# Context mixer of layer 0 and latent mixer of layer 1: scans woven with independent projections, attention with three branches of the merge

## What is computed

```
def token_mixer(h, hc, ...):
    conv, ret, mls, att, gate = split_cols(h @ w_in)
    y0 = silu(layernorm(depthwise_conv(a * sigmoid(g), 31 taps)))
    y1 = head_norm(retention forward + backward) * silu(g)
    y2 = head_norm(mlstm forward + backward) * sigmoid(o)
    y3 = attention(q, k, v with the context's k, v and a sink)
    acc = sum_i sigmoid(gate_i) * (y_i @ w_branch[i])
    return acc @ w_out
```

## Time and profile before

| | |
|---|---|
| median of three runs | 6388.14 us (6384.92 to 6395.45) |
| span of the profiled execution | 6397.6 us |
| instructions | 64900 |
| TensorE matmul, VectorE, ScalarE, POOL busy | 65%, 50%, 11%, 43% |
| `c0`: convolution / up to attention blocks / attention blocks / first merge | 42 / 289 / 35 / 170 us |
| `l1`: convolution / up to attention blocks / attention blocks / first merge | 65 / 494 / 104 / 166 us |

### The profile page before, as it was taken

The page is one execution under the profiler, slowest core; times in us unless marked ns, Lnnn a source line. Parts: engine busy times, 40 slices in busy tenths (PEclk is TensorE's granted clock), DMA queues, the critical chain, the costliest instruction groups (busy, mean ns, idle before and its releaser), DMA issues. The chain is left out here.

```text
span 6397.6 us, 64900 instructions
## 1 busy us (share of the span) xinstructions
PE 4139.9 (65%) x23632; PEld 2474.1 (39%) x23632; DVE 3226.7 (50%) x7718; ACT 732.2 (11%) x1583; POOL 2759.8 (43%) x2606
## 2 busy tenths in 40 slices
PE   5789646667899785554454567887986743434447
PEld 3568523333566665221111114555875620000001
DVE  4321499755511585756645306444137866564440
ACT  1220101111210011000000001133110100000000
POOL 0000023555532144777777750000003577777775
PEclk8899877877999888665555578989998955555555
DMA  6445346789788499999999981110457999999999
GB/s 217 164 155 168 119 141 199 252 322 324 283 284 274 158 327 327 377 366 378 380 390 407 403 325 55 42 43 16 136 164 249 338 375 367 404 366 393 403 401 382
DMA packets 721231, 1739.23 MB, mean 272 GB/s; under 512 B 88912, under 2 KB 371408, under 8 KB 719248
## 3 DMA queue, kind: packets, MB, share of 16 engines
q0 software_dynamic: 380032, 1384.49, 57.1%
q1 hardware_dynamic: 314896, 304.03, 15.2%
q10 hardware_dynamic: 25984, 46.56, 2.0%
HBM read 1706.98 MB, written 27.89 MB: 271 GB/s over the span
## 5 line engine op out<-in xcount | busy, mean ns | idle before, releaser
L2692 POOL DMA_INDIRECT arena<-in_peer_u,arena x1280 | 1414.7, 1105 | 2519.1 <-DVE arena L1838 1245.0
L1081 PE MATMUL bank<-arena 128*32 128x256 f32 x10240 | 1202.3, 564 | 1372.1 <-DMA arena<-in_peer_v,arena 1366.4
L1940 DVE CUSTOM_DVE_ANT_0 arena<-arena 128x1024 f32<-128x1024 f32 x1280 | 1541.2, 1223 | 922.3 <-DMA arena<-in_peer_u,arena 907.5
L2692 POOL DMA_INDIRECT arena<-in_peer_v,arena x1280 | 1318.4, 1030 | 622.7 <-issue 319.2
L1081 PEld LDWEIGHTS bank<-arena 128*32 128x32 f32 x10240 | 251.9, 131 | 2270.8 <-DMA arena<-in_peer_v,arena 2173.8
L620 PE MATMUL bank<-arena 128*128 128x512 f32 (+1 forms) x1856 | 723.6, 549 | 109.4 <-issue 81.7
L989 PE MATMUL bank<-arena 128*128 128x256 f32 x2560 | 621.6, 399 | 156.0 <-issue 75.5
L989 PEld LDWEIGHTS bank<-arena 128*128 128x128 f32 x2560 | 508.9, 201 | 251.0 <-issue 152.2
L620 PEld LDWEIGHTS bank<-arena 128*128 128x128 f32 x1856 | 377.0, 207 | 436.1 <-issue 412.2
L995 PE MATMUL bank<-arena 128*128 128x256 f32 x1280 | 305.7, 382 | 0.0
L1042 PE MATMUL bank<-arena 128*128 128x256 f32 x1280 | 288.7, 389 | 19.4 <-issue 16.9
(11 more groups left out here) (265 smaller groups left out, 3900.9 us busy)
## 6 DMA issues: line engine op xcount, KB each, us to landing
arena<-in_w_in SPq DMA_DIRECT2D x152, 1024.0 KB, 6.9
arena<-in_mod_w POOLq DMA_DIRECT2D x20, 2048.0 KB, 11.5
arena<-in_peer_wq SPq DMA_DIRECT2D x40, 1024.0 KB, 6.0
arena<-in_w_branch SPq DMA_DIRECT2D x60, 512.0 KB, 6.6
arena<-in_w_out SPq DMA_DIRECT2D x20, 1024.0 KB, 7.8
arena<-in_peer_u,arena POOLq DMA_INDIRECT x1280
arena<-in_peer_v,arena POOLq DMA_INDIRECT x1280
arena<-in_w_branch SPq DMA_DIRECT2D x40, 256.0 KB, 8.5
```

The source lines that it names most:

```text
L1081: i = mm(banks[6 + g // 2][32 * j:32 * j + 32, (g % 2) * W:(g % 2 + 1) * W], G["ws"][:, g, 32 * m:32 * m + 32], G["row"][ROW_BUFFER["v", i ...
L1940: v.tensor_tensor_reduce(u, u, G["h2"][it % 2], 1.0, 0.0, ALU.mult, ALU.add, G["dots"][:, n:n + 1]).then_inc(*pr.step("dot", it, n))
L2692: fl.done(eng.indirect_dma_start(G["row"][x], None, table, bass.IndirectOffsetOnAxis(ids[:, n:n + 1], 0)), f"row_landed{x}", (kind + "_lan ...
```

## The change

Two passes, `c0` and `l1`, get another order (`woven`). New regions of the arena (`lay_low`, `lay_odd`, `GR_TOP`, `H2R_TOP`) let work of neighbouring stages lie side by side: both heads' projections, both mLSTM halves, attention inputs beside the last scan, and the merge's accumulator beside attention. The stages `ret1`, `rows` and `mls1` no longer exist there; their work belongs to the scan stage in which it is woven. Taps come in groups of four a row tile (8 instructions) instead of eight in `conv_tail`. `attn` is split into its inputs and its blocks, and the merge of the first half into the three branches that need no attention output and the fourth.

```
+WOVEN = ("c0", "l1")
...
 def pass_stages(p):
+    if woven(p):
+        s = ["norm", "conv", "ret0", "rets0", "rets1", "mlss0", "mlss1", "attn"]
+        return s + [f"{x}{f}" for f in range(len(halves_of(p))) for x in ("merge", "out", "query")]
...
+def weave(a, b, per):
+
+    due = 0.0
+    for cost in a:
+        yield cost
+        due += per
+        while due >= 1.0:
+            due -= 1.0
+            for cost in b:
+                yield cost
+                break
+    yield from b
...
+def units(p):
+
+    nb, rotated = p.n // P, 1 if p.t0 else 0
+    return dict(ret=12 + nb + 4 * rotated, scan=2 * nb + 4, mls=13 + nb, rows=2 + ROWS_LATER + nb, attn_in=9 + nb + 5 * rotated,
+                attn_mix=4 * nb + 2, merge=48)
...
+def merge_parts(p, f):
+
+    every = [(j, i) for j in range(D // W) for i in range(4)]
+    if woven(p) and f == 0:
+        return [x for x in every if x[1] < 3], [x for x in every if x[1] == 3]
+    return [every]
+
+
+def tap_parts(p):
+
+    return [(0, x) for x in range(4, 8)] + [(1, x) for x in range(8)] if woven(p) else \
+        [(0, 2), (0, 3), (1, 0), (1, 1), (1, 2), (1, 3)]
...
             def ret(p, h):
-                mn.stage((f"ret{h}", p.name))
+                if h == 0 or not woven(p):
+                    mn.stage((f"ret{h}", p.name))
...
             def normed(p):
+                if woven(p):
+                    yield from conv(p)
+                    u = units(p)
+                    taps = conv_tail(p)
+                    yield from weave(first(taps, 8), ret(p, 0), u["ret"] / 8)
+                    yield from weave(ret_scan(p, 0), weave(taps, ret(p, 1), u["ret"] / 7), (u["ret"] + 7) / u["scan"])
+                    yield from weave(ret_scan(p, 1), weave(rows(p), mls(p, 0), u["mls"] / u["rows"]), (u["mls"] + u["rows"]) / u["scan"])
+                    yield from weave(mls_scan(p, 0), mls(p, 1), u["mls"] / u["scan"])
+                    yield from weave(mls_scan(p, 1), attn_in(p), u["attn_in"] / u["scan"])
+                    yield from weave(attn_mix(p), merge_part(p, 0, merge_parts(p, 0)[0]), u["merge"] / u["attn_mix"])
+                    yield from tail(p, 0)
+                    return
```

More of the change, by code:

```diff
@@ L777, in rows @@
             def rows(p):
-                mn.stage(("rows", p.name))
+                if not woven(p):
+                    mn.stage(("rows", p.name))
                 M, pn, nb = mls_work(p), p.name, p.n // P
@@ L804, in mls @@
             def mls(p, h):
-                if h:
+                if h and not woven(p):
                     mn.stage((f"mls{h}", p.name))
@@ L980, in merge, with merge_part @@
                 mn.stage((f"merge{f}", p.name))
+                yield from merge_part(p, f, merge_parts(p, f)[-1])
+            def merge_part(p, f, part):
                 pn, half = p.name, slice(f * W, (f + 1) * W)
[L982 to L1001, removed]
@@ L1422, in rows @@
             def rows(p):
-                mn.stage(("rows", p.name))
+                if not woven(p):
+                    mn.stage(("rows", p.name))
+                given = 0
                 M, pn, nb, l = mls_work(p), p.name, p.n // P, p.l
@@ L1481, in rows @@
                 yield 0
-                for _ in range(ROWS_LATER):
+                for _ in range(ROWS_LATER - given):
                     yield 0
```

230 lines of the change are left out of this document (169 added, 61 removed).

## The result

The changed kernel took 6286.62 us (median of 4 runs, 6280.44 to 6302.99), the one before 6390.59 us beside it (4 runs). The ratio is 0.9835, 95% interval 0.9814 to 0.9856: 1.65% faster, 104 us by the medians, 109.3 us by the spans of the two profiled executions (6397.6 and 6288.3). The forecast was 145 us and 6243 us.

A forecast was written before the change was run, and what follows sets the result against it. Bound by latency between engines: 226 us of PE standing still or at lower clock in two passes. Gains 88.6 (layer 1) + 54.3 (context) + 5 (attention) = 148, taken as 145 off 6388.1: 6243 us, range 6202 to 6316.

The forecast's parts named there:

- (b): Second retention scan, gate rows, first mLSTM projection: gap 26.0 us in layer 1, 17.9 context; 9 and 7 to stay.
- (c): First mLSTM scan and second projection: gap 30.8 us in layer 1, 21.4 context; 13 and 9 to stay.
- (d): Second mLSTM scan and attention inputs: gap 28.3 us in layer 1, 20.3 context; 13 and 9 to stay.
- Covered: all L1337 waits: Head norm at the end of scans: weaving hides all PE waits for it, 22.7 and 23.2 us in the two passes.
- (a): Retention projections, convolution tail, first scan: gap 51.5 us in layer 1, 29.7 context; 13 and 10 to stay.
- the convolution's border: Wait behind the two tap groups inside the convolution stage: unchanged, 11.8 us in layer 1.
- The taps: Convolution taps in groups of 8: layer 1 5.4 us against 8.6 of PE; 7.7 us wait goes, 3 us lag charged.
- Context pass: Layer 0's context pass: gap of 89.3 us before attention, of which 54.3 us would be gained.
- The border from the scaling of K: Before each mLSTM scan PE still waits for K's scaling: 5.0 us each in layer 1, 3.6 in the context pass.
- Attention: Three merge branches woven into attention: gain 3 us in layer 1, 2 in context; diagonal's wait stays once per step.
- The bank mechanism: Rival, chance 0.02: woven scan and attention steps wait for a PSUM bank's reader; 1.5 us a step costs 162, 6405 us.
- on the path: Rival, chance 0.03: ScalarE's Exp and Sigmoid table switches in woven attention lose 72 us of the gain, 6315 us.

The follow-up runs named there:

- late_turn: Changed kernel with TensorE's woven pieces before the last transposition of a retention scan step, ScalarE moving that result one step later: 6265.6 us.
- inside_whole: Changed kernel with merge pieces between attention's values and the transposition of the probabilities, each gate kept with its branch: 6237.1 us.
- inside: Changed kernel with merge pieces between attention's values and the transposition of the probabilities, pieces still cut between gate and branch: 6294.7 us.

## Why the prediction was right, and where not

The direction and the range held (6286.6 in 6202 to 6316), and the middle was too high by a third or more: 145 us forecast, 104 to 109 measured. By the experiments the woven scans earned 69.1 us (23.1 + 46.0), the taps 39.9, borders and layout 14.1, and attention lost 14.6; the forecast gave 142.9 to the first three together and +5 to attention. By its own steps:

- **What bounds.** Right: PE's pauses and the lower clock behind them were what there was to win. The clock rose nearly as said (0.93 or more in all but (b) and (c) of the context pass, 0.91 and 0.92).
- **Scans woven.** (c) and (d) kept 13 us each in layer 1 by the forecast; 84.9 and 78.7 us against 76.2 and 66.7 of work is 8.7 and 12.0. Right in kind and nearly in size. The failed sentence is "Covered: all L1337 waits": it holds for the mLSTM scans, whose turn comes a unit after its head norm, and for the context pass, not for the retention scans of layer 1, where head norm and transposition stand in one unit. The same structure that I had read for attention's diagonal I did not look for here. 18.0 us stayed; late_turn gave 21 us by the medians, 16.0 of them in the two retention stretches.
- **(a) and (b).** Forecast residue in layer 1: 13 and 9 us. Measured 160.7 - 137.5 = 23.2 and 97.9 - 77.0 = 20.9 us, the latter with the border of 5.0 us that I had put into (c). This is the shortfall before attention (74.4 us won where 88.6 were forecast), and more than all of it: (c) and (d) kept some 5 us less than forecast, and the convolution's border, which I called unchanged, gave 5.3 us.
- **The taps.** Right that 8.6 us of projection pieces outlast a group of 5.4; what they are worth by themselves I had not separated: 17.1 of 48.7 us in the context pass and 22.8 of 74.4 in layer 1, about a third of each.
- **Context pass.** 48.7 us against 54.3. The border from the scaling of K was taken as 3.6 us and was 7.8: I priced the wait but did not name what ScalarE would have queued in front of it, the store of the state with its wait for landing. The store of the second scan did the same at the next border, 6.1 us that no term of the sum named.
- **Attention.** I gave it +5 us and called its wait for the diagonal kept. The wait was kept (21.3 us), but the balance was -14.6 us. I had charged nothing for cut pieces. The bank mechanism stood among the rivals as one that must hold at every step to matter; it held at five and cost 12 us of waits; taking the cuts out gave 15.9 us in layer 1. In the context pass the forecast of 2 us won was right in kind: against the same layout without the weave it won 3.1 us.
- **Table switches.** The rival "on the path" (72 us) is out: inside_whole keeps 32 loads in layer 1 and runs blocks and merge in 246.3 us. The Trainium skill, page ScalarE: Activation LUTs, section "What ACT_TABLE_LOAD costs", gives about 2.66 us a switch, of which 1.38 are a drain, and the estimate of 149 us if all lay on the path came from it. No drain shows in this trace: the sigmoid starts 0.01 us after its load ends (4334.41 + 1.28, then 4335.70), and the load starts 0.02 us behind the instruction before it. So the measurement decides, and a switch cost 1.28 us here. Nor was the load on the path of inside_whole, under some 11 us of PE a step. In the changed kernel the loads did help to delay the sigmoid that held the bank; without cut pieces that delay is free.
- **DMA.** Right that no load would be late: none is among PE's waits at 187 to 230 GB/s in (a) to (d). But the small stores landed later, in the middle of that traffic (last section).

## To carry to other kernels

When independent work is woven between the steps of a latency-bound chain, it hides only waits whose two ends lie in different steps: look for pairs (VectorE result, TensorE consumer) within one step and put the filler between them, on the engine that waits. Do not cut a piece of filler between an allocation and its reader where the main work takes as many buffers as the ring has less one (7 of 8 in layer 1's steps); where it takes fewer (4 in the context pass) the cut cost nothing here, and whole pieces were worse. And at each border name what every in-order engine has queued in front of its last operation, a wait for a store above all.

## What the runs showed that was not expected

A state store of 129 KB landed in 2.4 us (median of 4) in the kernel before and in 6.9 us in the changed one, in the same pass. In the kernel before, each pair of stores had the DMA engines to itself: the 0.26 MB moved between 315 and 318 us, and again between 382 and 385, are the stores', which landed after 2.7 and 2.4 us. In the changed kernel the weight loads of both queues were under way at that time: the engines moved 265 GB/s over 305.8 to 313 us and 398 GB/s over 355 to 363, and the stores landed after 6.4 and 7.5 us. That this traffic is the cause is the plain reading, but no kernel tried it by itself.

With a cut piece, `inside` also had a mean clock of 0.93 against 0.99 in inside_whole, and PE's busy time was 256.90 us for the same matmuls against 242.59: waits of 4 to 6 us cost a second time through the clock. Beside each of the six waits of 3.9 to 6.2 us in that stretch the granted clock stood at the lower of its two levels (0.50 over 4348 to 4354.8 us, for one, beside the wait that ends at 4349.73); in inside_whole the longest wait of the stretch is 3.6 us, at its start.
